# Selector rows of two causal attentions, made from one tile that holds upper bits on the first partitions and lower bits from partition 32

## The reference, cut to what matters

```python
def mlstm_mixer(h, w_in, b_gate, w_head_norm, w_out):      # 8 heads
    ...
        b = jnp.cumsum(ft, axis=-1)
        dmat = jnp.where(causal, b[..., :, None] - b[..., None, :] + it[..., None, :], -jnp.inf)
        m_inter = b + m[..., None]
        m_t = jnp.maximum(m_inter, jnp.max(dmat, axis=-1))
        s = jnp.einsum('bhtd,bhsd->bhts', qt, kt) * jnp.exp(dmat - m_t[..., None])
        ...
def fox_mixer(h, w_qg, w_out, k, v, c):                    # 16 heads
    ...
        logits = jnp.einsum('bqhd,bkhd->bhqk', qi, k).astype(jnp.float32)
        logits = logits + (ci[..., :, None] - c[..., None, :])
        ...
        p = jax.nn.softmax(logits, axis=-1)
```

## Time and profile before

| what | value |
|---|---|
| time, median of 3 runs | 2633.58 us (2631.14 to 2635.16) |
| span of the profiled execution | 2636.9 us |
| instructions in it | 31348 |
| PE busy | 2533.4 us, 96% |
| DVE busy | 1537.5 us, 58% |
| ACT busy | 1027.1 us, 39% |
| mean granted TensorE clock | 0.981 |

### The profile page before, as it was taken

One profiled execution on the slowest core, in us unless ns is written; L12 is line 12 of the kernel. 1 busy time (PEld: TensorE's weight loads), 2 busy tenths in 40 slices (PEclk: granted clock), 3 DMA queues, 4 the chain that ended last, 5 costly groups with the idle time before them and its releaser, 6 DMA issues.

```text
span 2636.9 us, 31348 instructions
## 1 busy us (share of the span) xinstructions
PE 2533.4 (96%) x12464; PEld 2006.7 (76%) x12464; DVE 1537.5 (58%) x2568; ACT 1027.1 (39%) x1581; POOL 96.2 (4%) x133
## 2 busy tenths in 40 slices
PE   7999999999999989999998998999999998999998
PEld 6887788887776667888876875788888665788887
DVE  6455676867455656646565256666653897534433
ACT  4344543424435555434245235323223324422323
POOL 0000001010000000000000000011100110000000
PEclk9999999999999999999999999999999999999999
DMA  5322335464221122333324220366652221233331
GB/s 171 112 81 80 88 97 171 147 177 134 66 88 49 55 69 77 96 96 96 92 74 136 72 73 17 116 196 193 191 158 88 64 65 33 87 96 96 96 98 54
DMA packets 285080, 266.86 MB, mean 101 GB/s; under 512 B 13331, under 2 KB 270663, under 8 KB 284935
## 3 DMA queue, kind: packets, MB, share of 16 engines
q1 hardware_dynamic: 268503, 210.33, 26.0%
q0 software_dynamic: 15024, 54.33, 7.0%
q10 hardware_dynamic: 1408, 0.20, 0.0%
HBM read 262.72 MB, written 2.10 MB: 100 GB/s over the span
## 4 chain that ended last, share of the span: by engine, by line
PE 86%; DVE 8%; ACT 3%; issue 2%; SPq 1%; DMA 0%; POOL 0%; ACTq 0%; DVEq 0%; POOLq 0%
PE G L2277 70%; PE G L2293 7%; DVE Y L2097 2%; PE M L2345 1%; DVE S L2097 1%; DVE w_lo L502 1%; PE M L1143 1%; PE M L798 1%; PE M L808 1%; PE M L2327 1%; PE M L1618 1%; PE M L1154 1%; PE M L1165 1%; PE M L1607 0%; ACT w_hi L497 0%
## 5 line engine op out<-in xcount | busy, mean ns | idle before, releaser
L502 DVE TENSOR_TENSOR w_lo<-raw,w_hi 128x1024 fp32r<-128x1024 f32 x396 | 482.8, 1224 | 675.2 <-ACT w_hi L497 674.3
L2277 PE MATMUL G<-H_hi,w_hi 128*128 128x512 f32 (+1 forms) x2016 | 808.4, 401 | 20.2 <-DVE H_lo L365 12.0
L2277 PE MATMUL G<-H_lo,w_hi 128*128 128x512 f32 (+1 forms) x2016 | 788.5, 391 | 0.0
L2277 PE MATMUL G<-H_hi,w_lo 128*128 128x512 f32 (+1 forms) x2016 | 788.4, 391 | 0.0
L497 ACT ACTIVATE w_hi<-raw 128x1024 fp32r<-128x1024 f32 x396 | 417.2, 1056 | 935.8 <-PE G L2277 828.4
L2277 PEld LDWEIGHTS G<-H_hi,w_hi 128*128 128x128 f32 x2016 | 383.5, 190 | 127.3 <-issue 46.1
L2277 PEld LDWEIGHTS G<-H_hi,w_lo 128*128 128x128 f32 x2016 | 382.9, 190 | 80.6
L2277 PEld LDWEIGHTS G<-H_lo,w_hi 128*128 128x128 f32 x2016 | 383.5, 190 | 79.4 <-issue 4.7
L2277 PE MATMUL G<-hid_hi,w_hi 128*128 128x512 f32 x864 | 339.4, 393 | 7.5 <-DVE hid_lo L621 4.7
L2277 PE MATMUL G<-hid_lo,w_hi 128*128 128x512 f32 x864 | 338.5, 392 | 0.0
L2277 PE MATMUL G<-hid_hi,w_lo 128*128 128x512 f32 x864 | 338.5, 392 | 0.0
(11 more groups left out here) (329 smaller groups left out, 2390.4 us busy)
## 6 DMA issues: line engine op xcount, KB each, us to landing
raw<-in_w_ff SPq DMA_DIRECT2D x128, 512.0 KB
mod_w<-in_w_mod POOLq DMA_DIRECT2D x96, 512.0 KB, 4.5
raw<-in_ffn_w_up SPq DMA_DIRECT2D x176, 256.0 KB
raw<-in_ffn_w_down SPq DMA_DIRECT2D x40, 512.0 KB
raw<-in_w_in SPq DMA_DIRECT2D x28, 512.0 KB
raw<-in_mlstm_w_in SPq DMA_DIRECT2D x24, 512.0 KB
raw<-in_kv_w SPq DMA_DIRECT2D x16, 512.0 KB
raw<-in_fox_w_qg SPq DMA_DIRECT2D x16, 512.0 KB
```

Of the source, the lines that this page charges most:

```text
L502: dve.tensor_tensor(w_lo[:, j, :], raw[:, j, :], w_hi[:, j, :], ALU.subtract).then_inc(lo_done, 1)
L2277: mm = pe.matmul(G[:, 2 * p + m, 0:n], lw[:, k, ms], rh[:, t, 0:n], start=(t == 0 and q == 0), stop=(t == st["ktiles"] - 1 and q == 2), sk ...
```

## The change

The upper and the lower bits of a row now lie in one tile: the upper bits on the first partitions, the lower bits from partition 32 on, zeros between. The selector `sel_x` has 48 partitions, with an identity at 0 and another at 32, so that one product adds both parts. Fox's two products for each head become one of 48 partitions. The mLSTM's float32 product becomes one fp32r product of 40 partitions, for which its rows are now split as well: DVE copies the upper bits (`m_high`), subtracts them, clears 32 partitions and copies the upper bits in. `sel_x` is made in the mLSTM part; the fox part clears 32 partitions of `x_row` in its place.

```diff
-        sel_x = small("sel_x", [16, 16], F32R)
+        sel_x = small("sel_x", [48, 16], F32R)
...
-        x_row = at("x_row", 172 * K, [16, 2, T], F32R)
+        x_row = at("x_row", 172 * K, [48, T], F32R)
+        m_row = at("m_row", 200 * K, [40, T], F32R)
+        m_high = at("m_high", 138 * K, [8, T], F32R)
...
-                pe.matmul(M[:, 0, :], ident[0:8, h:h + 1].to_broadcast([8, P]), root[0:8, :], start=True,
+                pe.matmul(M[:, 0, :], sel_x[0:40, h:h + 1].to_broadcast([40, P]), m_row[:], start=True,
                           stop=True).then_inc(ml["bc"], 1)
...
-            dve.scalar_tensor_tensor(root[0:8, :], log_row[0:8, :], 0.5, root[0:8, :], ALU.mult, ALU.add).then_inc(row_c, 1)
+            dve.tensor_copy(sel_x[0:32, :], ident[0:32, 0:16])
+            dve.tensor_copy(sel_x[32:48, :], ident[32:48, 32:48])
+            link(dve.scalar_tensor_tensor(root[0:8, :], log_row[0:8, :], 0.5, root[0:8, :], ALU.mult, ALU.add))
+            link(dve.tensor_copy(m_high[:], root[0:8, :]))
+            link(dve.tensor_tensor(m_row[32:40, :], root[0:8, :], m_high[:], ALU.subtract))
+            link(dve.memset(m_row[0:32, :].bitcast(F32), 0.0))
+            dve.tensor_copy(m_row[0:8, :], m_high[:]).then_inc(row_c, 1)
...
-                chosen = sel_x[:, h:h + 1].to_broadcast([16, P])
-                for part in range(2):
-                    mm = pe.matmul(M[:, 3, :], chosen, x_row[:, part, :], start=(part == 0), stop=(part == 1))
-                mm.then_inc(fx["bc"], 1)
+                pe.matmul(M[:, 3, :], sel_x[:, h:h + 1].to_broadcast([48, P]), x_row[:], start=True,
+                          stop=True).then_inc(fx["bc"], 1)
...
-            act.activation(x_row[:, 0, :], rows[0:16, 4, :], ACT.Copy, scale=-1.0).then_inc(row_c, 1)
+            act.activation(x_row[0:16, :], rows[0:16, 4, :], ACT.Copy, scale=-1.0).then_inc(row_c, 1)
...
-            dve.tensor_copy(sel_x[:], ident[0:16, 0:16])
+            link(dve.memset(x_row[0:32, :].bitcast(F32), 0.0))
...
-            dve.scalar_tensor_tensor(x_row[:, 1, :], rows[0:16, 4, :], -1.0, x_row[:, 0, :], ALU.mult,
+            dve.scalar_tensor_tensor(x_row[32:48, :], rows[0:16, 4, :], -1.0, x_row[0:16, :], ALU.mult,
                                      ALU.subtract).then_inc(row_c, 1)
```

## The result

The changed kernel takes 2621.26 us (median of 5 runs, 2618.05 to 2623.16) against 2634.83 us (5 runs, 2631.14 to 2636.44) of the kernel before: a ratio of 0.9943, 95% interval 0.9932 to 0.9955. Two later comparisons, each on one chip, gave 0.9961 (0.9948 to 0.9974) and 0.995 (0.9936 to 0.9964). It is faster, as forecast, but by 10.0 to 13.6 us between the medians of the three comparisons, where 8.0 us were forecast; 2621.26 us lies at the very edge of the range. The profiled execution has a span of 2621.3 us (before 2636.9 us), with the same mean clock of 0.981.

The account below looks back on a forecast made before the run. PE was taken to bound the kernel, busy 96% of the span with 86% of the chain. Savings of 4.4 us (mLSTM) and 3.6 us (fox), DVE additions free, made 8.0 us: 2633.6 to 2625.6 us, range 2621.0 to 2630.0 us.

Parts of the forecast that it names:

- mLSTM, 7 x 0.63 = 4.4 us: mLSTM heads on PE: rows 0 to 6 each fall from 1.05 to 0.42 us in the chain, 4.4 us saved.
- Row 7: Last mLSTM row, at 215.04 us: saves nothing, as the chain lies on ACT; 0.6 us if ACT were not late.
- Fox, 16 x 0.23 = 3.6 us: Fox steps on PE: sixteen rows each lose one product at the 0.23 us pace, 3.6 us saved.
- the remainder of 0.20 us: Around fox's pair of products: 0.65 us less 0.45 us at the pace, laid to operand change, paid once per row.
- What is added on DVE: New DVE instructions ahead of the mLSTM rows, 2.5 us, and fox's clearing for a cast: costed at nothing.
- the cover: Slack of 5.1 us between ACT's exponential, done at 57.44 us, and PE's need at 62.57 us; hides 2.5 us delay.
- The rival of the cheap product: Mlstm and fox rows: the single product is cheaper than 0.42 us, giving 2621.1 us; chance 0.06.
- rival that the clock takes back part: Half-clock stretches after PE idles may shift; two more places losing 1.7 us each give 2629.0 us, no change; chance 0.09.

Follow-up runs that it names:

- the last run: Changed kernel with mLSTM and fox selector rows each one product of all 128 partitions, zeros where no bits lie: 2617.47 us, 0.9927 to the kernel before.
- mLSTM alone: Changed kernel with fox put back to two products of 16 partitions: 2632.36 us, 0.9993 to the kernel before; again 2632.89 us, 0.9993.
- fox alone: Changed kernel with the mLSTM row put back to a float32 product of 8 partitions: 2628.68 us, 0.9981 to the kernel before; again 2630.16 us, 0.9975.

## Why the forecast was too small

**mLSTM, 7 x 0.63 = 4.4 us: right.** The pieces are 0.43 us. Between the product at 84.01 us and the one at 214.09 us of before, the second and third profile of the kernel after lose 4.3 us each. The first loses 5.9 us (130.08 to 124.19 us), since it is also spared the slow clock from 106 us on: twelve products take 2.95 us there, and took 4.54 us before. Row 7 is not in the chain, and the last rows end in ACT's work at 210.43 us as forecast. The number is right by luck in part: the forecast saw no difference between products of 16 and of 128 partitions, and the last run has 0.24 us for this row at 128.

**Fox, 16 x 0.23 = 3.6 us: the step that failed.** The sum over the sixteen rows fell by 20.73 - 15.09 = 5.64 us. Its parts: two rows between projections give 0.23 us each, fourteen rows ahead of scores give 0.43 us each, together 6.5 us; one of these waits for DVE and gives back 0.6 us, and behind the last row the value products start 0.2 us later, for which the trace names no cause. I priced the row by itself, from a row that has weight products on both sides (777.64 to 779.74 us), and carried the price to fourteen rows that have scores behind them. The earlier trace rows show what to ask: at the last row the scores start 0.65 us behind the row, so they had been waiting for it.

What was wrong is the remainder of 0.20 us. The forecast put it down to the change of operands and had every row pay it once. It goes with the height: padded to 128 partitions, with new operands all the same, the row between projections costs 0.236 us and has no remainder. Ahead of scores a pair of 16 partitions has a change of height on both sides; the change makes the row 48 partitions high, and towards the scores nothing changes any more. So these rows save the product, 0.23 us, and a change of height, 0.20 us. The run with one product of 16 saves the first and not the second, the run with two products of 48 the second and not the first, and the run with 128 partitions both, without a score beside the row.

The Trainium skill has it in "TensorEngine Tiling (Array Packing)", section "Key Properties": a change of the tiling mode drains TensorE, and different tiles can load weights and multiply in parallel. That the height of a product sets the mode here is read from the runs. With it the traces agree with both: 0.2 us at each change of height, and 0.01 us from row to score where they lie on different halves. By the first rule a row of 128 partitions between products of 128 needs no drain, and the last experiment agrees, with 0.24 us for the row.

**What is added on DVE: right.** The delay is 2.6 us, the cover hides it. In fox the clearing stands where DVE waits anyway:

```profile
732.72 0.48 DVE L1359 MEMSET x_row<- 32x512 f32 x1 [0.16 <-DVE rows L1358]
...
736.82 1.23 DVE L504 TENSOR_TENSOR w_lo<-raw,w_hi 128x1024 fp32r<-128x1024 f32 x1 [3.62 <-ACT w_hi L499]
```

DVE is idle for 3.62 us ahead of the next weight piece, against 4.00 us in the earlier trace rows; the edit is free.

**The range.** With fox at 5.65 us the sum is 4.3 + 5.65 = 10.0 us, 2623.6 us from the median before. That stands inside the range, and the two later comparisons (10.0 and 12.6 us between medians) go with it or a little beyond. The rival of the cheap product, 2621.1 us, meets the number but not the cause: the rows cost 0.43 us, not 0.23. That 2621.26 us still lies inside the range is luck: 3.6 us of the distance between the first medians are not in the rows.

**What goes beyond 10.0 us: the clock, in part open.** The spans of the two first profiles differ by 15.6 us. Cut at the same products, the kernel after loses 1.7 us up to 84 us, gains 5.9 us in the mLSTM (1.6 of them at 106 us), 1.4 us between the attentions, 5.6 us in fox, 0.1 us up to the product at 1360 us of before, 7.9 us from there to the one at 1458 us, and loses 3.7 us behind it. The largest piece that is not in the rows lies far behind both attentions. The chain of waits of before there:

```profile
1424.95 9.11 PE M L2345 x16
...
1447.39 2.68 PE G L1498 x64
...
1450.74 9.31 PE G L2277 x30
```

And after:

```profile
1410.12 7.52 PE M L2351 x16
...
1430.96 2.11 PE G L1504 x64
...
1433.74 22.06 PE G L2283 x96
```

The same sixteen products take 9.11 or 7.52 us, the same 64 take 2.68 or 2.11, the thirty behind them 0.31 us each and then 0.23. In the table by stretch the granted clock is 0.83 on average from 1440 to 1460 us before, between its levels of 1.2 and 2.4 GHz, and 1.00 after. In both PE stood still in between, twice for some 4 us, while a transfer into `sel` landed. No instruction there was changed, and mLSTM alone has 7.52 us for the sixteen products in one profile and 9.10 us in the other. The forecast's rival that the clock takes back part was the right place to look, with the sign open; here it gave.

Whether the clock gives on average is not settled. The halves, timed alone, are 1.8 us (mLSTM, both times, with intervals that include no change) and 5.0 and 6.6 us (fox) by their ratios; their profiles show 5.9 us in the mLSTM stretch (4.3 of the rows and the 1.6 at 106 us, both times) and 5.65 us in fox. Runs of the mLSTM half spread over 10.9 and 10.7 us, so that what it lacks may lie in which executions meet the slow clock where; no run here tells. One thing speaks for a share of the change: behind fox, from the same product (at 941 us of before) to the last, the four profiles with the old fox rows take 1686.5 to 1690.3 us and the ten with new ones 1682.4 to 1686.0 us. But each is one execution, and the times of fox alone, 5.0 and 6.6 us, leave no room for as much beside its 5.65 us.

## What to carry to other kernels

Price a product by what it borders on: what counts is the distance from the product ahead to the product behind, and at each change of height (16, 40 to 64, or 128 partitions in these runs) that distance grows by about 0.2 us here. A small product between tall ones is cheapest when padded to their height (0.24 us at 128 partitions, 0.43 us at 40), and beside a single product of half height it is cheapest on the other half (0.63 us for both against 0.86 us). When executions of one program differ by 4 us, check a forecast of 8 us in the stretches that the edit touches, not in the span alone.

## What the runs showed of the hardware

- A row on partitions 0 to 47 and a score on partitions 64 to 127 start 0.01 us apart; with a row of 16 partitions it is 0.42 us, with a row of 40 or 48 and a score on partitions 0 to 63 it is 0.33 us.
- Rows of 16, 40 and 48 partitions all cost 0.425 to 0.43 us between products of 128; one of 128 costs 0.236 us. With the gaps on both sides a row of 128 saves 0.39 us over one of 40, for two changes of height.
- A score with its own operands started ahead of a row product that stands before it in the program (0.02 us behind the first of two, where the second followed 0.34 us later).
- The same sixteen products took 7.5 or 9.1 us in different executions, by the granted clock, at a place that no edit here touches.
